# Rotary scores of the latent attention as two float32r products with halves stacked on the rows, in a two-layer hybrid trunk

## What is computed

```python
q = rms_norm((rms_norm(q_lat, q_lat_norm) @ w_q_up).reshape(B, S, H, 192), q_norm)
k = rms_norm(concat([k_nope, broadcast(k_rope)]), k_norm)
q = concat([q[..., :128], rotary(q[..., 128:], cos, sin)])
k = concat([k[..., :128], rotary(k[..., 128:], cos, sin)])
s = einsum('bqhd,bkhd->bhqk', q_block, k) * 192 ** -0.5   # blocks of 128 queries
s = where(key_chunk <= query_chunk, s, -1e30)             # chunks of 64
out = softmax(s) @ v
```

## Time and profile before

| | |
|---|---|
| median of 3 runs | 1432.56 us (1432.38 to 1434.05) |
| profiled execution | 1433.42 us, span 1431.7 us |
| granted TensorE clock, mean | 0.998 |
| TensorE busy | 1413.5 us (99%) |
| weight loads (overlap the products) | 1159.4 us (81%) |
| VectorE, ScalarE, GpSimd busy | 770.4, 622.2, 667.3 us |
| chain that ended last | 95% TensorE |

### The profile page before, as it was taken

One profiled execution on the slowest core, in us unless ns is written; L12 is line 12 of the kernel. 1 busy time (PEld: TensorE's weight loads), 2 busy tenths in 40 slices (PEclk: granted clock), 3 DMA queues, 4 the chain that ended last, 5 costly groups with the idle time before them and its releaser, 6 DMA issues.

```text
span 1431.7 us, 17072 instructions
## 1 busy us (share of the span) xinstructions
PE 1413.5 (99%) x6677; PEld 1159.4 (81%) x6677; DVE 770.4 (54%) x1120; ACT 622.2 (43%) x1077; POOL 667.3 (47%) x370
## 2 busy tenths in 40 slices
PE   8999999999999999999999999999999999999999
PEld 6888778887788888888878877888778888888887
DVE  5584665565785305653165655737557661166621
ACT  6647482655432212322346555735754332232321
POOL 4645653552444444444346367535334444544443
PEclk9999999999999999999999999999999999999999
DMA  6331012332242333323333310213223332333322
GB/s 175 89 103 60 30 36 69 118 103 60 74 118 89 98 93 104 103 88 96 91 89 103 89 60 15 74 60 118 89 59 89 106 100 89 100 92 102 103 85 91
DMA packets 174207, 125.64 MB, mean 88 GB/s; under 512 B 12561, under 2 KB 150576, under 8 KB 174128
## 3 DMA queue, kind: packets, MB, share of 16 engines
q1 hardware_dynamic: 173568, 124.55, 29.2%
q10 hardware_dynamic: 560, 0.01, 0.0%
HBM read 122.44 MB, written 2.10 MB: 87 GB/s over the span
## 4 chain that ended last, share of the span: by engine, by line
PE 95%; ACT 2%; DVE 1%; DMA 1%; issue 1%; POOL 0%; SPq 0%
PE bank L626 28%; PE bank L630 27%; PE bank L628 27%; PE bank L948 2%; PE bank L779 2%; PE bank L908 1%; PE bank L909 1%; PE bank L990 1%; PE bank L767 1%; ACT cprobs L1174 1%; DMA x_tok<-in_x 1%; PE bank L887 1%; PE bank L845 0%; PE bank L1065 0%; ACT cprobsT L1187 0%
## 5 line engine op out<-in xcount | busy, mean ns | idle before, releaser
L552 POOL TENSOR_TENSOR w_lo<-raw,w_hi 128x1024 fp32r<-128x1024 f32 (+1 forms) x230 | 547.8, 2385 | 681.4 <-ACT w_hi L1131 681.4
L1131 ACT ACTIVATE w_hi<-raw 128x1024 fp32r<-128x1024 f32 (+1 forms) x230 | 237.6, 1035 | 339.9 <-PE bank L630 336.4
L626 PE MATMUL bank<-x_hi,w_hi 128*128 128x512 f32 (+1 forms) x944 | 371.5, 394 | 1.3 <-issue 1.2
L628 PE MATMUL bank<-x_lo,w_hi 128*128 128x512 f32 (+1 forms) x944 | 367.9, 390 | 0.0
L630 PE MATMUL bank<-x_hi,w_lo 128*128 128x512 f32 (+1 forms) x944 | 367.9, 390 | 0.0
L626 PEld LDWEIGHTS bank<-x_hi,w_hi 128*128 128x128 f32 (+1 forms) x944 | 177.0, 187 | 42.6 <-issue 4.5
L628 PEld LDWEIGHTS bank<-x_lo,w_hi 128*128 128x128 f32 (+1 forms) x944 | 177.0, 187 | 38.6 <-issue 1.4
L630 PEld LDWEIGHTS bank<-x_hi,w_lo 128*128 128x128 f32 (+1 forms) x944 | 176.9, 187 | 37.7
L1889 DVE SCALAR_TENSOR_TENSOR conv<-gate_in,gains_all,conv 128x512 f32<-128x512 f32 x44 | 120.2, 2733 | 1.6
L1482 ACT ACTIVATE conv_silu<-conv 128x512 f32<-128x512 f32 x44 | 27.8, 632 | 169.8 <-DVE conv L1890 169.8
L1617 DVE TENSOR_TENSOR h<-h,bank 128x512 f32<-128x512 f32 x48 | 31.8, 681 | 110.7 <-PE bank L630 110.6
(11 more groups left out here) (314 smaller groups left out, 2295.4 us busy)
## 6 DMA issues: line engine op xcount, KB each, us to landing
raw<-in_w_ffn_in SPq DMA_DIRECT2D x88, 512.0 KB, 3.8
raw<-in_w_ffn_out SPq DMA_DIRECT2D x40, 512.0 KB, 3.7
raw<-in_w_in SPq DMA_DIRECT2D x28, 512.0 KB, 3.8
raw<-in_w_mix_out SPq DMA_DIRECT2D x16, 512.0 KB, 3.7
raw<-in_w_ca_kv SPq DMA_DIRECT2D x32, 256.0 KB, 3.3
raw<-in_w_in SPq DMA_DIRECT2D x18, 256.0 KB, 3.0
raw<-in_w_ca_q SPq DMA_DIRECT2D x8, 512.0 KB, 3.7
raw<-in_w_ca_out SPq DMA_DIRECT2D x8, 512.0 KB, 3.8
```

The costliest lines, as they stand in the source:

```text
L552: pool.tensor_tensor(w_lo[gi % SPLIT][:, 0:n], raw[gi % RAW][:, 0:n], w_hi[gi % SPLIT][:, 0:n].bitcast(f32), ALU.subtract).then_inc(S["lo_ ...
L626: pe.matmul(o, ah, bh, start=first, stop=False)
L628: pe.matmul(o, ah, bl, start=False, stop=False)
L1131: act_.activation(w_hi[k % SPLIT][:, 0:n], raw[k % RAW][:, 0:n], ACT.Copy).then_inc(S["hi_split"], 1)
```

## The change

The rotary product of a head is split. `qT_r` becomes float32r: the head's own 64 rows hold the high half, and the 64 rows that were zero hold the low half. `kT_r` becomes float32r with one plane for each head, in which both row halves hold the key's high half; the key's low half goes to a new `kT_l`, a pair of heads per 128 rows as before. `mla_score` issues three products: nope in float32 as before, then (high and low query) by (high key) on 128 rows, then high query by low key on the head's 64 rows alone.

The zeros of POOL go away. ACT copies the rotary rows of the keys in two copies of 64 rows, as it did for the queries. DVE gets a new routine `qkT_low`: for a query block two subtractions on 64 rows, for a key block two copies (of the high half onto the other 64 rows) and two subtractions. The rotary bank is freed by the new semaphore `qkT_lo` instead of `qkT_evac`, and the scores of a block wait for that block's `qkT_evac` and `qkT_lo`, where the whole attention waited for all sixteen `qkT_evac` and for `zeroed`. Since `kT_r` and `kT_l` need more room, the homes of several operands in the arena change; no transfer and no other instruction does.

```diff
-        qT_r = place("qT_r", R1 + 16, [P, NH, SEQ])
-        kT_r = place("kT_r", R3, [P, 2, SEQ])
+        qT_r = place("qT_r", R1 + 16, [P, NH, SEQ], f32r)
+        kT_r, kT_l = place("kT_r", R3, [P, NH, SEQ], f32r), place("kT_l", R3 + 8, [P, 2, SEQ], f32r)
...
-        ya_hi, ya_lo = place("ya_hi", R3 + 4, [P, NH, SEQ], f32r), place("ya_lo", R3 + 12, [P, NH, SEQ], f32r)
-        yb_hi, yb_lo = place("yb_hi", R1 + 8, [P, NH, SEQ], f32r), place("yb_lo", R1 + 16, [P, NH, SEQ], f32r)
+        ya_hi, ya_lo = place("ya_hi", R1, [P, NH, SEQ], f32r), place("ya_lo", R1 + 8, [P, NH, SEQ], f32r)
+        yb_hi, yb_lo = place("yb_hi", R3 + 8, [P, NH, SEQ], f32r), place("yb_lo", R1 + 16, [P, NH, SEQ], f32r)
...
-                        if i == SPLIT - 1:
-
-                            for half in range(2):
-                                pool.memset(qT_r[:, 2 * half:2 * half + 2, :], 0.0).then_inc(S["zeroed"], 1)
...
-                            freed[b + 1] = (S["qkT_evac"], past(layer, "qkT_evac") + 2 * (z * NT + t) + 2)
+                            freed[b + 1] = (S["qkT_lo"], past(layer, "qkT_lo") + z * NT + t + 1)
...
-                    pe.wait_ge(S["qkT_evac"], past(layer, "qkT_evac") + 4 * NT)
                     pe.wait_ge(S["v_evac"], past(layer, "v_evac") + NT)
 
-                    pe.wait_ge(S["zeroed"], past(layer, "zeroed") + 2)
-
                     def mla_score(o, hd, t, n):
+                        if hd == 0:
+                            pe.wait_ge(S["qkT_evac"], past(layer, "qkT_evac") + 2 * (NT + t) + 2)
+                            pe.wait_ge(S["qkT_lo"], past(layer, "qkT_lo") + NT + t + 1)
                         pe.matmul(o, qT_n[:, hd, t * P:(t + 1) * P], kT_n[:, hd, 0:n], start=True, stop=False)
-                        return pe.matmul(o, qT_r[:, hd, t * P:(t + 1) * P], kT_r[:, hd // 2, 0:n], start=False, stop=True)
+                        pe.matmul(o, qT_r[:, hd, t * P:(t + 1) * P], kT_r[:, hd, 0:n], start=False, stop=False)
+                        rows_ = slice(ROPE * (hd % 2), ROPE * (hd % 2 + 1))
+                        return pe.matmul(o, qT_r[rows_, hd, t * P:(t + 1) * P], kT_l[rows_, hd // 2, 0:n], start=False, stop=True)
...
-                            if z:
-                                ev = act_.activation(dr[:, :, t * P:(t + 1) * P], two, ACT.Copy)
-                            else:
-                                for r in range(2):
-                                    half = slice(ROPE * r, ROPE * (r + 1))
-                                    ev = act_.activation(dr[half, r::2, t * P:(t + 1) * P], two[half], ACT.Copy)
+                            for r in range(2):
+                                ev = act_.activation(dr[halves[r], r::2, t * P:(t + 1) * P], two[halves[r]], ACT.Copy)
...
+                    def qkT_low(z, ts):
+                        for t in ts:
+                            two = pb[2 * (t % 2) + 1][:, 0:2 * P].rearrange("p (r q) -> p r q", r=2)
+                            halves = slice(0, ROPE), slice(ROPE, 2 * ROPE)
+                            dve.wait_ge(S["qkT_evac"], past(layer, "qkT_evac") + 2 * (z * NT + t) + 2)
+                            if z:
+                                for r in range(2):
+                                    dve.tensor_copy(kT_r[halves[1 - r], r::2, t * P:(t + 1) * P], two[halves[r]])
+                            for r in range(2):
+                                half, other = halves[r], halves[1 - r]
+                                hi = (qT_r, kT_r)[z][half, r::2, t * P:(t + 1) * P].bitcast(f32)
+                                lo = kT_l[half, :, t * P:(t + 1) * P] if z else qT_r[other, r::2, t * P:(t + 1) * P]
+                                ev = dve.tensor_tensor(lo, two[half], hi, ALU.subtract)
+                            ev.then_inc(S["qkT_lo"], 1)
+
+                    qkT_low(0, (0, 1))
+
                     dve.wait_ge(S["f_sig"], past(layer, "f_sig") + 1)
...
                     dve.tensor_scalar(Q[:, 1:3, :], Q[:, 1:3, :], HDK ** -0.5, None, ALU.mult).then_inc(S["q_scaled"], 1)
+                    qkT_low(0, (2, 3))
+                    qkT_low(1, range(NT))
```

More of the change, by code:

```diff
@@ L258, in build_trunk @@
         decay_x = place("decay_x", R3 + 20, [P, 3, SEQ // 2])
-        o_tok = place("o_tok", R1, [P, NT, 512])
-        k_hat = place("k_hat", R1 + 8, [P, 3, NT, P])
-        state = place("state", R1 + 14, [P, NT - 1, 512])
+        o_tok = place("o_tok", R3, [P, NT, 512])
+        k_hat = place("k_hat", R3 + 8, [P, 3, NT, P])
+        state = place("state", R3 + 14, [P, NT - 1, 512])
         o_sq = place("o_sq", R1 + 20, [P, 2, 512])
@@ L271, in build_trunk @@
         mem_tok = place("mem_tok", R0, [P, MT, D])
-        m_hi, m_lo = place("m_hi", R1, [P, KD, NM], f32r), place("m_lo", R5 + 4, [P, KD, NM], f32r)
+        m_hi, m_lo = place("m_hi", R3, [P, KD, NM], f32r), place("m_lo", R5 + 4, [P, KD, NM], f32r)
         ckv_tok = place("ckv_tok", R2, [P, MT, D])
[L274 to L277, removed]
+        ckv_sq = place("ckv_sq", R1, [P, MT, NH, P])
+        ckT = place("ckT", R1 + 4, [P, NH, NM])
+        cq_tok = place("cq_tok", R1 + 8, [P, NT, NH * P])
+        cqT = place("cqT", R1 + 16, [P, NH, SEQ])
         cq_sq = place("cq_sq", R4, [P, NT, NH * P])
@@ L308, in build_trunk @@
             lat_mm lat_evac lat_sq_done lat_sq_sum lat_hi_done lat_lo_done lat_ss_mm r_lat_done
-            rope_mm rope_lr_done rope_t rope_evac q_mm q_evac k_mm k_evac v_mm v_evac qk_ss qk_r qk_done qkT_mm qkT_evac
+            rope_mm rope_lr_done rope_t rope_evac q_mm q_evac k_mm k_evac v_mm v_evac qk_ss qk_r qk_done qkT_mm qkT_evac qkT_lo
             feat_mm feat_evac f_sig q_silu tok_mm tok_evac gate_mm gate_exp gate_min gate_done
@@ L397, in build_trunk @@
             silu_done=2 * FC, a_hi_done=FC, x_lo_done=3 * KD, r_bc_done=2, lat_evac=4, rope_lr_done=1,
-            lat_lo_done=4, feat_evac=len(FEATS), qk_ss=2 * NT, qk_done=2 * NT, kr_done=1, q_scaled=1, gate_min=1, score_max=20,
+            lat_lo_done=4, feat_evac=len(FEATS), qkT_lo=2 * NT, qk_ss=2 * NT, qk_done=2 * NT, kr_done=1, q_scaled=1, gate_min=1, score_max=20,
             probs_done=20, q_level=2 * len(LEVELS) + 4, pv_lo=2 * NH, swept=4 * len(LEVELS), state_done=NT - 1, o_ss=NT,
@@ L1354, in attention_between @@
                         if i == EXPANDS:
-                            act_.wait_ge(S["zeroed"], past(layer, "zeroed") + 4)
+                            act_.wait_ge(S["zeroed"], past(layer, "zeroed") + 2)
                             act_.wait_ge(S["q_level"], past(layer, "q_level") + 4)
@@ L1373, in _ @@
                                 if li == 0:
-                                    act_.wait_ge(S["zeroed"], past(layer, "zeroed") + 6 + x)
+                                    act_.wait_ge(S["zeroed"], past(layer, "zeroed") + 4 + x)
                                 else:
@@ L1804, in _ @@
                                 dve.copy_predicated(odd_blocks(pair, m), mask, bank).then_inc(S["swept"], 1)
-                    dve.wait_ge(S["zeroed"], past(layer, "zeroed") + 5)
+                    dve.wait_ge(S["zeroed"], past(layer, "zeroed") + 3)
                     for n in range(NT - 1):
```

2 lines of the change are left out of this document (1 added, 1 removed).

## The result

The changed kernel takes 1437.69 us (median of 6 runs, 1435.84 to 1442.85), the kernel before 1433.28 us (6 runs, 1432.24 to 1434.71): ratio 1.0036, 95% interval 1.0022 to 1.0049. The ratio is the record's estimate and not the quotient of the two medians, which is 1.0031. The kernel is slower: the whole interval lies above 1.002. The forecast was 1437.9 us.

What follows compares the result with a forecast made beforehand. TensorE was taken to bound the kernel: -17.3 + 10.1 + 12.8 - 0.4 = +5.2 us, called +5.3 with small handovers. Added to 1432.6 this gave 1437.9 us, range 1434.5 to 1441.

Steps and rivals of the forecast that it cites:

- TensorE bounds the attention: Attention: TensorE has no free time, so each us of it is one of the kernel; others count only if it waits.
- Columns: -17.3 and +10.1 us: Attention scores on TensorE: removed float32 rotary product saves 17.3 us; two new float32r products cost 10.1 by their columns.
- The rival of slow short float32r products: Score products: those of 128 columns run like float32 ones, 2.2 us on top, 1440.1 us; chance 0.08.
- The change of the row count: 64 x 0.20 - 0.4 = 12.4 us: Around 32 64-row score products: 0.20 us each way, 12.8 us, less 0.4 where the 128-column floor doesn't apply.
- the gate's 0.20: At the gate, a 16-row product between float32r products: 0.40 us missing, read as 0.20 us per row-count change each way.
- The rival that 64 rows cost nothing: Score products: the 64-row product slots in like a 128-row one, a gain of 7.2 us, 1425.4 us; chance 0.08.
- The rival of a partial overlap: Row-count changes at the score products overlap in part, 0.13 us each, 8.3 in all: +0.7 us, 1433.3 us; chance 0.05.
- ScalarE and GpSimd: 0: ScalarE's split key copies (2 us more a layer) and GpSimd's removed memsets hold up nothing on TensorE: 0.
- VectorE: 0, with up to 0.3 us a layer at bank 3: Before the attention: 24 new instructions a layer, about 0.35 us each, just free rotary bank 3 for the last key block.
- waits of TensorE for VectorE at L846: Key transposes: waits of TensorE for VectorE here in the changed kernel's profile were named as showing the prediction wrong.
- VectorE blocked by GpSimd: Rival, key block 2's low half: GpSimd's 3.51 us product delays VectorE, 1.2 us a layer, 2.4 in all, 1440.3; chance 0.07.
- Homes and looser waits: 0: New operand homes change no instruction's size; looser waits for qkT_evac release nothing, since TensorE didn't wait there: 0.

Runs made afterwards that it cites:

- The later transposes: The changed kernel with the transposes of key block 3 put after the first two tokens of the last bvr step; 1437.23 us (1.0038), second set 1437.43 us (1.0040).
- the experiment with bank 3: The changed kernel with VectorE's subtractions first, freeing the rotary bank, and the high-half copies then reading SBUF; 1442.39 us, ratio 1.0063.
- the grouped form: The changed kernel with each head's 64-row products of query blocks 0 and 1 issued side by side; 1444.53 us (1.0073), second set 1441.40 us (1.0067).

## Why the prediction was right

The forecast of +5.3 us stands against +4.4 in the medians and +4.4 in the traces at equal clock. Part of this agreement is luck: the medians of the three sets differ by 4.4, 2.4 and 6.4 us (the ratios, 1.0034 to 1.0041, are steadier), and the forecast of 1437.9 us comes within 0.2 of the measured time because it was 0.9 us too high in the change and started from a time 0.7 us too low for the kernel before (1432.56 against 1433.28). By its steps:

- **TensorE bounds the attention.** Right: in the changed kernel it never waits there, and each us of its work is one of the kernel. It is right in this direction only. With a shorter TensorE part (low product on 128 rows, or left out) it waits for the softmax, and only a part of the saving arrives (3.6 of 5.4 us a layer with 128 rows).
- **Columns: -17.3 and +10.1 us.** The two sets measure 1.24 us a head by ends in the run on 128 rows (0.58 for the high set, 0.66 for the low) where 1.26 was said; 9.9 us. The floor of 0.11 us for 128 columns held for a product behind another float32r one (0.12), not behind the float32 nope product (0.06). The rival of slow short float32r products falls.
- **The change of the row count: 64 x 0.20 - 0.4 = 12.4 us.** Right as to the mechanism, shown in both directions: removed it gives 0.18 us a change back, added alone to the kernel before it costs 0.18. The term was too large. What is left of the attention's +3.4 us is 3.4 + 17.3 - 9.9 = 10.8 us, 0.17 each; the gate's 0.20 was for a float32 product of another form, and ahead of the transposes of the probabilities, where 18 of the 32 changes out stand, one costs 0.15 us (by ends, the first transpose takes 0.26 us behind a 64-row product and 0.11 behind one of 128 rows). The rival that 64 rows cost nothing falls. The rival of a partial overlap, 8.3 us at 0.13 each, got a chance of 0.05 and was not far off: the 10.8 us lie between it and the 12.8 of the sum. The Trainium skill, TensorEngine Tiling (Array Packing), section Tiling Modes, says that changing the tiling mode drains the engine. The trace agrees: the loads at 129.97 and 131.29 start only when the product before has all but run out.
- **ScalarE and GpSimd: 0.** Right; nothing of TensorE's waits leads to them in the changed kernel's attention.
- **VectorE: 0, with up to 0.3 us a layer at bank 3.** The place was right, the size wrong: 0.35 us was said for an instruction of 64 rows and 256 columns, halved from one of 512 columns; it takes 0.43. So block 1's four end at 125.53 in place of about 124.9 on this trace's clock, and TensorE loses 0.47 us a layer. The later transposes remove just this. The prediction had named waits of TensorE for VectorE at L846 as a sign of being wrong, and this sign did show: not for the mechanism that decides the result, but for the nothing that stood in the sum at this place.
- **VectorE blocked by GpSimd.** It wasn't, for what reads a bank (0.86 for two instructions under GpSimd's product of 3.5 us from 126.11). It is for copies from SBUF to SBUF, as the experiment with bank 3 shows.
- **Homes and looser waits: 0.** Right for the homes (1.0004). The looser waits were not run alone; TensorE waits for no `qkT_evac` in either trace.

The two misses, -2 us in the attention and +0.9 us at bank 3, partly cancel. Not foreseen at all was the clock. Of 28 runs of the changed kernel 17 lie between 1434.86 and 1438.38 us and 11 between 1442.05 and 1444.77, while the 73 runs of the kernel before all lie between 1431.87 and 1435.04. The median falls where it does by the share of the two groups.

## What to carry to other kernels

In these runs a product on 64 rows of the array was not cheaper than one on 128, and between products on all rows it cost 0.15 to 0.2 us on the way in and again on the way out: fill the other rows, or put all of a kind together. On 128 rows, two float32r products beat one float32 product here (ratio 0.9972). That run adds a small foreign term to the scores, however; to keep them exact the other 64 rows would have to hold zeros, which was not tried. And what waits next is the softmax, so the slack of such a chain has to be read before a gain is summed. Where TensorE's work is thin, compare profiles at equal clock, stage by stage: the median alone hid the 1.2 us a layer that the grouped form saves on TensorE.

## What the runs showed of the hardware

TensorE's clock fell to its lower level where the engine was not idle (3.40 us busy of 3.40 in the window up to 144.4, where it fell). In the attention it did so fourteen times, in seven profiles of six kernels, each time at the end of a group of 24 products of 2 or 4 columns (L883, L886 or L887) between filler products, or within 1 us behind it; at 758.1 us in the kernel before, and near 52 us in three profiles (two of the changed kernel, one of the grouped form), it did so 1 to 2 us behind the sixteen products of one column. Twice more it fell behind the wait of 1.9 us for VectorE (bank 3 freed early). Six profiles also have such a stretch from 11 or 12 us on, at the start, behind TensorE's wait for its input: in these six it waits 2.35 to 2.80 us for `x_tok` there, in the seven others 1.81 to 2.11 us. The stretches were 3.4 or 6.8 us long and cost 1.7 and 3.1 us. The kernel before with new homes fell at the same place as the changed kernel, for 3.4 us instead of 6.8. Which groups bring it about isn't settled: the same groups stand in both profiles of the changed kernel that kept the full clock there (59.60 us each). That the 64-row products make the long stretches more likely was not shown: the kernel without a low-key product had one too, at 859 us.
